# Plain matmuls of the identity by constants added ahead of TensorE's waits in the first part of a decoder-step kernel

## The reference, cut to what matters

```python
n1 = rmsnorm(x, norm1_g)
proj = n1 @ w_in                  # q,k,v of the window attention, q,k,v,gates of the GLA
oa = banded_swa(qa, ka, va, attn_sinks)
log_a = log_sigmoid(zb @ w_gla_gate + b_gla_gate) / GATE_TEMP
og, S_new = gla_recurrent(qg, kg, vg, log_a, S0, 64)
og = rmsnorm(og, gla_norm_g) * silu(rb)
u = sigmoid(ga) * oa + sigmoid(gb) * og
x = x + u @ w_out
x = x + peer(rmsnorm(x, norm2_g), peer_wq, peer_subkeys, peer_u, peer_v)
```

## Time and profile before

| | |
|---|---|
| runs | 3481.46, 3485.74, 3486.98 us; median 3485.74 |
| the profiled execution | 3483.83 us, span 3482.0 us, mean granted clock of PE 0.888 |
| busy over the span | PE 80%, DVE 78%, POOL 56%, ACT 21% |
| part 0 | from 0 to about 403 us; first gather issued at 406.25 us |
| chain that ended last, by engine | DVE 29%, PE 27%, DMA 22%, POOL 9%, issue 8% |

### The profile page before, as it was taken

The page is one execution under the profiler, slowest core; times in us unless marked ns, Lnnn a source line. Parts: engine busy times, 40 slices in busy tenths (PEclk is TensorE's granted clock), DMA queues, the critical chain, the costliest instruction groups (busy, mean ns, idle before and its releaser), DMA issues.

```text
span 3482.0 us, 33342 instructions
## 1 busy us (share of the span) xinstructions
PE 2775.3 (80%) x9955; PEld 1759.1 (51%) x9955; DVE 2733.2 (78%) x5958; ACT 738.7 (21%) x1781; POOL 1933.0 (56%) x1820
## 2 busy tenths in 40 slices
PE   8889779888797989789999677978878756555555
PEld 7777767556663656454665354645656312111111
DVE  0641798997889868977889999889778878777776
ACT  1321123332211123323111112322210111101011
POOL 0000167777667757766666777777776744333332
PEclk9899889999899999899999898998989977777777
DMA  4224589999999999999999999999999999999997
GB/s 157 73 73 164 198 351 420 419 415 406 421 420 420 420 393 420 356 335 386 420 421 420 375 417 415 420 409 399 415 421 420 419 400 427 427 427 427 427 427 319
DMA packets 303219, 1297.19 MB, mean 373 GB/s; under 512 B 33352, under 2 KB 42592, under 8 KB 250016
## 3 DMA queue, kind: packets, MB, share of 16 engines
q0 software_dynamic: 260352, 1082.25, 76.3%
q1 hardware_dynamic: 42688, 212.81, 15.5%
HBM read 1279.34 MB, written 17.66 MB: 372 GB/s over the span
## 4 chain that ended last, share of the span: by engine, by line
DVE 29%; PE 27%; DMA 22%; POOL 9%; issue 8%; DVEq 3%; ACT 1%; ACTq 1%; PEldq 0%; PEld 0%; SPq 0%; POOLq 0%
PE banks L1055 9%; DVE ringb L1586 8%; DMA ringb<-in_uv,eidx 8%; PE vsum L972 8%; POOL ringb L788 7%; DVE acc L1639 5%; DMA ringb<-in_v,eidx 3%; DMA wring<-in_uv,eidx 3%; PE banks L1097 2%; DVE scT L2045 2%; PE n2p L1055 2%; PE banks L1255 2%; DMA qkb<-in_uv,eidx 1%; DMA wring<-in_w 1%; DMA arena<-in_uv,eidx 1%
## 5 line engine op out<-in xcount | busy, mean ns | idle before, releaser
L972 PE MATMUL vsum<-ringb,diag 128*128 128x512 f32 x1700 | 927.7, 685 | 305.1 <-ACT diag L1307 189.4
L788 POOL DMA_INDIRECT ringb<-in_u,eidx x655 | 710.5, 1085 | 737.2 <-DVE eidx L1720 431.0
L1586 DVE SCALAR_TENSOR_TENSOR ringb<-ringb,n2p 128x1024 f32<-128x1024 f32 x825 | 980.6, 1216 | 152.5 <-DMA ringb<-in_uv,eidx 97.0
L788 POOL DMA_INDIRECT ringb<-in_v,eidx x656 | 716.0, 1092 | 275.4 <-issue 179.1
L972 PEld LDWEIGHTS vsum<-ringb,diag 128*128 128x128 f32 x1700 | 342.0, 214 | 779.3 <-issue 425.9
L1055 PE MATMUL banks<-wring,nTb 128*128 128x256 f32 (+1 forms) x2768 | 626.3, 386 | 26.5 <-DMA wring<-in_w 23.8
L1055 PEld LDWEIGHTS banks<-wring,nTb 128*128 128x128 f32 (+1 forms) x2768 | 496.9, 181 | 159.3 <-DMA wring<-in_w 29.5
L1639 DVE SCALAR_TENSOR_TENSOR acc<-ringb,wgt,acc 128x1024 f32<-128x1024 f32 x316 | 405.0, 1282 | 18.9 <-DMA ringb<-in_v,eidx 15.7
L1307 ACT ACTIVATE diag<-cst,wgt 128x128 f32<-128x128 f32 x535 | 204.4, 397 | 856.7 <-DVE wgt L1602 604.6
L771 POOL DMA_INDIRECT ringb<-in_uv,eidx x170 | 159.9, 941 | 265.7 <-DVE banks L1639 126.6
L1097 PE MATMUL banks<-nTb,wring 128*128 128x256 f32 (+1 forms) x1056 | 239.1, 384 | 4.9 <-DMA wring<-in_w 2.8
(11 more groups left out here) (421 smaller groups left out, 3579.3 us busy)
## 6 DMA issues: line engine op xcount, KB each, us to landing
wring<-in_w SPq DMA_DIRECT2D x152, 1024.0 KB, 7.7
ringb<-in_v,eidx POOLq DMA_INDIRECT x656, 15.4
ringb<-in_u,eidx POOLq DMA_INDIRECT x655, 13.5
n2t<-scratch_n SPq DMA_DIRECT2D x14, 512.0 KB, 6.5
bTb<-in_keysT SPq DMA_DIRECT2D x4, 1024.0 KB, 11.8
vgb<-in_xp SPq DMA_DIRECT2D x4, 1024.0 KB, 8.9
arena<-in_s SPq DMA_DIRECT2D x8, 512.0 KB, 7.4
out_ss<-arena SPq DMA_DIRECT2D x8, 512.0 KB, 12.8
```

The lines of the kernel that those rows point to most:

```text
L788: pool.indirect_dma_start(out=ring[r], out_offset=None, in_=a["u"] if kind == "u" else a["v"], in_offset=place)\
L972: last = mm(out[:, g * 512:(g + 1) * 512], lhs, row[:, g * 512:(g + 1) * 512], start=(x == first), stop=(x == end))
L1586: STT(row, row, 1.0, n2, ALU.mult, ALU.mult, accum_out=dg[:, m % 2, at:at + 1]).then_inc(used(("u", x))[0], 1)
```

## The change

A helper `warm(ps, n)` issues n matmuls, 128 x 128 identity by the first 512 columns of the constants, each complete in itself (start and stop), with no wait and no signal. All of them write the first of `vsum`'s two banks (`ps[:, 0:512]`). Nothing reads what they write before PE's first real sum starts the bank anew. They are issued in part 0 only, ahead of seven kinds of wait:

```diff
+            def warm(ps, n):
+                for _ in range(n):
+                    mm(ps[:, 0:512], ident, cst[:, 0:512], start=True, stop=True)
...
                     if 1 <= n <= NQ:
                         m = n - 1
+                        if c == 0:
+                            warm(vsum, 5 if m == 0 else 1)
                         pe.wait_ge(p_ready.sem, p_ready.at((c, m)))
...
                     beside("gla", n, 0)
+                    if c == 0 and n == len(gla_units(c)) - 1:
+                        warm(vsum, 16)
                     pe.wait_ge(k_ready.sem, k_ready.at((c, n)))
...
                     beside("gla", n, 2)
+                    if c == 0:
+                        warm(vsum, 2)
                     emptied(pe, ("kdT", c, n))
                     for j in range(nt):
                         v = vog[:, t0 + j, h * DV:(h + 1) * DV]
                         ps = room(pe, ("og", c, n, j))
+                        if c == 0:
+                            warm(vsum, 3)
                         pe.wait_ge(sc_ready.sem, sc_ready.at((c, n, j)))
...
                 beside("mg", 0)
+                if c == 0:
+                    warm(vsum, 4)
                 pe.wait_ge(u_ready.sem, u_ready.at(c))
...
                 beside("n2", 1)
+                if c == 0:
+                    warm(vsum, 12)
                 for t, R in tiles_of(c):
                     pe.wait_ge(n2_ready.sem, n2_ready.at((c, t)))
```

## The result

| | before | after |
|---|---|---|
| runs | 3480.86 to 3487.28 us, median 3485.74 (5) | 3493.82 to 3502.04 us, median 3500.15 (5) |
| ratio | | 1.0035, 95% interval 1.0018 to 1.0052 (+6 to +18 us) |
| profiled execution, span | 3483.83, 3482.0 us | 3493.82, 3492.0 us |
| first gather issued | 406.25 us | 415.13 us |

The change costs about 14 us. The profiled execution after is the lowest of its five, so the two profiles differ by 10.0 us and not by 14. One execution of all those reported here, of the kernel before, took 3619.07 us at a mean granted clock of 0.786 instead of 0.89; the ratios leave it out.

A forecast was written before the change was run, and what follows sets the result against it. Before the first gather PE mostly bounds the kernel, afterwards DMA. Added calls of 65.3 us against about 32 us of waits, with about 16 us won by the clock, gave +14.7 us: 3499 us, range 3484 to 3510.

The forecast's parts named there:

- the first rival: PE's waits before the first gather hide the added calls, at 0.43 us each: lag -12.7, 3471 us; chance 10%.
- 2, L of unit 0: Ahead of GLA unit 0: two single added calls cost +1.7 us, bringing the lag to +0.3.
- 3, scores behind unit 0: Inside GLA unit 0: added calls outlast their waits; first product +2.5 us late, second +3.0.
- 4, O behind them: Scores and vb after unit 0: 9.0 us at full clock instead of 12.03, so -3.0 and lag 0.
- 5, O behind unit 1: Two single calls +1.7 us, unit 1 to +2.9, then scores and vb at full clock bring -1.0.
- 6, end of unit 2: Two single calls bring +0.7 us; unit 2, already at full clock, adds +3.0 for eight calls: lag +3.7.
- 7, L of the last unit: Ahead of the last GLA unit: sixteen calls overrun the 8.42 us wait by 6.1 us, lag +9.8.
- 8, ga units: Last GLA unit: eight calls cost +2.6 us net of 1.5 won by clock; lag +12.4, carried to 308 us.
- 10, first query: Second norm: twelve calls, 10.3 us, for 6.5 us of wait, +3.7; about 1.0 comes back, lag +14.7.
- The carry: Delay before the first gather reaches the end nearly whole, the DMA engines having no slack afterwards: 14.7 us.
- Taking a share of the delay back: Same overrun before the first gather, but 5 to 12 us absorbed, there or later: 3487 to 3494 us; chance 13%.
- The clock that falls anyway: Before the first gather the 16 us aren't won and some 20 calls cost 0.86 more: 3532 us; chance 6%.

The follow-up runs named there:

- fitted kernel: 70 calls of 256 columns, counts cut to the waits of the kernel before, added to that kernel: 3471.83 us, ratio 0.9954.
- doubled kernel: Every count of added calls in the changed kernel doubled, to 152 calls of 512 columns: 3565.0 us.

## Why the prediction was right, point by point

**Price of a call.** Right: 0.86 us, two records, as the earlier trace rows said. The half-width and 384-column kernels show that this number decides the sign, and that the break-even lies at the 0.65 us a call that the first rival named. For 0.43 us a call the prediction's walk ended 12.7 us ahead of before; the half-width kernel is 12 us faster.

**The walk.** Lag against before, counted from the second scores in the first pair of profiles (measured is the difference of starts plus 2.77):

| step | predicted | measured |
|---|---|---|
| 1, first O | -1.4 | -1.3 |
| 2, L of unit 0 | +0.3 | +0.3 |
| 3, scores behind unit 0 | +3.0 | +2.4 |
| 4, O behind them | 0 | -0.7 |
| 5, O behind unit 1 | -1.0 | -2.5 |
| 6, end of unit 2 | +3.7 | +1.4 |
| 7, L of the last unit | +9.8 | +7.4 |
| 8, ga units | +12.4 | +9.5 |
| 9, wo units | +12.0 | +9.3 |
| 10, first query | +14.7 | +11.6 |

No step has the wrong sign against this profile. The lag at the end was put 3.1 us too high. Some 2.3 us of it arose in steps 3 to 6: from unit 0's second product to the scores behind it 1.39 us pass, not the 1.75 of before, which the walk carried over; unit 1 cost 0.7 us net of the clock, not 1.2; and unit 2 cost 2.3 us, not 3.0. Steps 8 and 10 added another 0.5 and 0.4.

In absolute times the signs that I had named all came early: L of the last unit at 217.15 us for 222, the ga units at 232.13 for 237.8, the first query matmul at 362.10 for 368, the first gather at 415.13 for 421. The shorter first 98 us are 2.8 us of that, the rest is the lag. The 152 records are there, the last one at 358.9 us, and no half clock between 97 and 400 us.

The table flatters the walk, though, since it compares with the very profile that the walk was read from. Against the second profile of before step 4 reads +0.9, step 5 +4.4 and step 7 +13.1, for the half-clock stretches at 137 and 164 us that the walk won back in steps 4 and 5 are not in it. The end reads +13.8, so only the sum carries over: the lag was 0.9 to 3.1 us too high.

**The single calls** cost nearly their full 0.86 us in steps 2, 5 and 6 (1.6 us for two) where the units' calls make PE the late engine; alone, ahead of unit 0, two of them cost 0.25 us. The prediction didn't say on what that term hung.

**The clock.** I took about 16 of at most 17.5 us, on one profile. The fitted kernel gives 15.3 against that profile and 13.1 against the second one. The bound from PE's busy time in the half-clock stretches was a good one. The Trainium skill's product of throttled time and one minus the ratio ("TensorE: Matmul & The Clock Gate", section "Terms") gave 22.1 us, and no run here reached it: it counts stretches in which PE had nothing to do. What I had wrong is that each stretch has its fixed place. That my sum held although two of the stretches in it moved is partly luck.

**The carry.** Right in size: 65.3 us more in part 0 came out as 65 us at the end. But the end isn't a clean measure of a few microseconds. From the first gather to the end the 14 profiles took from 3075.8 to 3085.8 us, with no clear relation to part 0. The first gather moved by 8.9 us in the first pair of profiles, and from a mean of 404.2 (two profiles of before) to 414.6 (two of after), by 10.4. The medians moved by 14.4 in one comparison and by 13.0 in the other, each with an interval of 5 us or more either side. So that the median met my 14.7 within 0.3 us is partly chance: the lag was 1 to 3 us too high, and the scatter of the rest filled it.

**The rivals.** Hiding all calls falls: the waits held 33.9 us, I had said about 32, and 65.3 were added. Taking a share of the delay back falls with the doubled kernel. For a fixed 5 to 12 us of slack nothing speaks: from the first gather to the end the two profiles of before took 3075.8 and 3082.1 us, the two of the changed kernel 3076.9 and 3078.9, and the medians moved by more than the first gather did, not by less. The clock that falls anyway is false for this change, but it is what happens with 16 partitions.

## What to carry to other kernels

Before filling PE's waits with spare matmuls, price one call in the data type at hand from a row, and count records: a float32 call of 512 columns was two of them, 0.86 us, and at half that price the same change would have been a gain. Fit each filling to its own wait, and check afterwards that the waits still stand in the list with a little left; once they have gone, every further call is paid in full. The same filling at half the length was 12 us faster than the kernel before, at full length 14 us slower. Take more than one profile before pinning a clock loss to a wait.

Work ahead of a wait can be free or dear depending on which engine is late there, so parts tried alone don't add up: the units' calls alone cost 12 us, the single calls alone gained 11 to 13, and together with the rest they made 14 us of loss. Eight single calls brought nearly as much as 70 fitted ones, and the runs don't say why.

## What the runs showed of the hardware that I had not expected

- A PE occupied all the time can still be at half clock: 328.0 of 329.4 us busy at clock 0.81 with calls on 16 partitions, 261.9 of 263.7 us at clock 1.00 with calls on 128.
- The places of the half-clock stretches differ between executions of one program (137 and 164 us in one, 187 us in the other), while the distance around them differed by 2.2 us.
- The clock column can miss the first microseconds: in the first profile of before it says 1.00 from 9 to 20 us, but the first 32 projection records took 9.14 us, where the same 32 took 7.14 after. The second scores start between 97.36 and 102.03 us in the 14 profiles, with the same work ahead of them.
